# Sliding-window attention in a fused encoder step: probabilities divided ahead of their transposes, values as the stationary side, one pipeline stage more, and staging and sums on GpSimd

## What is computed

```python
def sink_attention(q, k, v, mask, sink):
    s = einsum('bnqhgd,bnkhd->bnhgqk', qg, k) * (HEAD_DIM ** -0.5)
    s = where(mask, s, -inf)
    mx = maximum(max(s, -1), sk)
    p = exp(s - mx)
    p = p / (sum(p, -1) + exp(sk - mx))
    o = einsum('bnhgqk,bnkhd->bnqhgd', p, v)
```

## Time and profile before

| | |
|---|---|
| Time, median of 3 runs | 2906.19 us (2901.15 to 2909.29) |
| Time of the profiled execution | 2909.79 us |
| Its span | 2908.0 us, 39590 instructions |
| TensorE's mean granted clock | 0.976 of full |
| Attention: first scores to the start of the output projection | 271.9 to 410.6 us |

### The profile page before, as it was taken

How to read it: one execution, slowest core, us unless ns; L and a number is a source line. 1 busy time by engine, 2 the same in 40 slices (tenths; PEclk the granted TensorE clock), 3 DMA queues, 4 the chain that set the end, 5 groups by cost and what they waited for, 6 DMA issues and landing times.

```text
span 2908.0 us, 39590 instructions
## 1 busy us (share of the span) xinstructions
PE 2795.7 (96%) x15799; PEld 2709.9 (93%) x15799; DVE 1076.5 (37%) x1476; ACT 541.0 (19%) x937; POOL 821.0 (28%) x584
## 2 busy tenths in 40 slices
PE   7999989999999999999899999989999999999995
PEld 7997769999999999999889898979999999999995
DVE  5127743422222221246645454552522222222225
ACT  3113631200110010022322314141201100100011
POOL 6542002322222222223122221342222222222231
PEclk9999979999999999999999999999999999999997
DMA  6321021111111111121233241432111111111111
GB/s 186 70 58 30 0 75 44 37 44 43 43 43 37 42 43 43 44 92 54 50 99 47 69 79 51 91 113 98 44 44 42 37 43 40 46 43 39 41 44 65
DMA packets 107099, 163.97 MB, mean 56 GB/s; under 512 B 55564, under 2 KB 66828, under 8 KB 106240
## 3 DMA queue, kind: packets, MB, share of 16 engines
q1 hardware_dynamic: 32368, 100.72, 12.5%
q10 hardware_dynamic: 74368, 60.93, 7.3%
q0 software_dynamic: 272, 0.98, 0.1%
HBM read 132.81 MB, written 24.49 MB: 54 GB/s over the span
## 4 chain that ended last, share of the span: by engine, by line
PE 84%; issue 9%; DVE 3%; POOL 2%; ACT 1%; DMA 0%; ACTq 0%; DVEq 0%; POOLq 0%
PE psum L572 76%; PE psum L671 2%; PE psum L794 1%; PE psum L599 1%; POOL w_lo L438 1%; PE psum L752 1%; PE psum L770 1%; POOL mid L522 1%; POOL w_hi L435 0%; PE psum L892 0%; DVE mid L1032 0%; DVE low L1526 0%; DVE a_lo L1169 0%; POOL mid L512 0%; PE psum L851 0%
## 5 line engine op out<-in xcount | busy, mean ns | idle before, releaser
L435 POOL TENSOR_SCALAR w_hi<-w_raw 128x1024 fp32r<-128x1024 f32 x191 | 204.5, 1071 | 1765.6 <-PE psum L572 1555.7
L572 PE MATMUL psum<-a_hi,w_hi 128*128 128x384 f32 x2808 | 655.4, 341 | 36.6 <-DVE a_lo L1020 16.9
L572 PE MATMUL psum<-a_lo,w_hi 128*128 128x384 f32 x2808 | 642.9, 336 | 0.0
L572 PE MATMUL psum<-a_hi,w_lo 128*128 128x384 f32 x2808 | 642.3, 336 | 0.0
L572 PEld LDWEIGHTS psum<-a_hi,w_hi 128*128 128x128 f32 x2808 | 502.0, 190 | 45.9 <-issue 22.8
L572 PEld LDWEIGHTS psum<-a_hi,w_lo 128*128 128x128 f32 x2808 | 505.1, 189 | 0.0
L572 PEld LDWEIGHTS psum<-a_lo,w_hi 128*128 128x128 f32 x2808 | 504.9, 189 | 0.0
L438 POOL TENSOR_TENSOR w_lo<-w_raw,w_hi 128x1024 fp32r<-128x1024 f32 x191 | 460.9, 2413 | 15.9
L1054 DVE TENSOR_TENSOR low<-psum,low 128x1152 f32<-128x1152 f32 x144 | 195.5, 1358 | 634.0 <-PE psum L572 633.9
L572 PE MATMUL psum<-h_hi,w_lo 128*128 128x384 f32 x1536 | 348.5, 334 | 0.0
L572 PE MATMUL psum<-h_hi,w_hi 128*128 128x384 f32 x1536 | 348.5, 334 | 0.0
(11 more groups left out here) (217 smaller groups left out, 2264.8 us busy)
## 6 DMA issues: line engine op xcount, KB each, us to landing
w_raw<-in_wall SPq DMA_DIRECT2D x191, 512.0 KB, 3.6
low<-in_x ACTq DMA_DIRECT2D x16, 576.0 KB, 9.0
high<-in_mem_in ACTq DMA_DIRECT2D x32, 257.0 KB, 4.7
out_mem_s<-high ACTq DMA_DIRECT2D x32, 257.0 KB, 3.1
out_x_spill<-low ACTq DMA_DIRECT2D x8, 576.0 KB, 2.7
low<-out_x_spill ACTq DMA_DIRECT2D x8, 576.0 KB, 7.0
out_y<-low ACTq DMA_DIRECT2D x8, 576.0 KB, 2.8
out_mix_spill<-mid ACTq DMA_DIRECT2D x3, 1152.0 KB, 5.4
```

What stands on the lines that cost most here:

```text
L435: nc.gpsimd.tensor_scalar(w_hi[:, s, :], w_raw[:, s, :], 1.0, 1.0, ALU.mult, ALU.mult)\
L572: r = mm(psum[:, z + i, 0:TN], w[:, s, k * P:(k + 1) * P], a[:, kk, tok(i)], start=first and n == 0, stop=last and n == 2)
```

## The change

Six edits go together. (1) The sums are finished on GpSimd (`denominators`), VectorE takes the reciprocal and multiplies the probabilities by it in place (`normalise`), before TensorE transposes them; `output` is gone. (2) In `weigh` the values are stationary with 64 columns and the transposed probabilities move, 128 columns; each key head writes its own half of the PSUM partitions, so that the result is already turned and `flip_out` is gone. (3) The sinks' exponentials take an argument that GpSimd has made (`sink_less_max`), so one activation does both heads. (4) `stage` moves to GpSimd, on all 128 partitions, with 0/1 masks in `halves`. (5) The stages stand at k = 0, 2, 3, 4 where they stood at k = 0, 1, 2, 3. (6) The steps are all written out.

The first three functions of the diff are GpSimd's, `normalise` is VectorE's, and the last activation is ScalarE's.

```diff
+            def stage(c, p):
+                n = 2 * c + p
+                if not first_two(n):
+                    pool.wait_ge(s_done, n - 1)
+                for v in range(2):
+                    r = nc.gpsimd.tensor_scalar(qs[:, v, 2 * p:2 * p + 2, :], qT[:, 2 * p:2 * p + 2, bass.ds(CH * c, CH)],
+                                                halves[:, v:v + 1], 1.0, ALU.mult, ALU.mult)
+                r.then_inc(q_staged, 1)
...
+            def sink_less_max(c, p):
...
+                pool.wait_ge(m_done, n + 1)
+                nc.gpsimd.tensor_tensor(st[:, p, 4:4 + width], st[:, p, 2:2 + width], cols[:, col:col + width], ALU.add)\
+                    .then_inc(sink_moved, 1)
...
+            def denominators(c, p):
...
+                pool.wait_ge(p_done, n + 1)
+                nc.gpsimd.tensor_tensor(st[:, p, 8:8 + width], st[:, p, 6:6 + width], st[:, p, 10:10 + width], ALU.add)\
+                    .then_inc(den_done, 1)
...
+                for k, part in ((-1, stage), (0, sink_less_max), (0, denominators)):
...
             def flip(c, p):
-                pe.wait_ge(p_done, n + 1)
+                pe.wait_ge(norm_done, n + 1)
...
-                    for v in range(2):
-                        for g, w, _, tile in parts:
-                            r = mm(psum[:, 6 + p, HD * v:HD * v + HD], pT[0:w, p, 2 * g + v, :],
-                                   v128[0:w, tile, HD * v:HD * v + HD], start=g == 0, stop=g == len(parts) - 1)
+                    for g, w, _, tile in parts:
+                        for v in range(2):
+                            h_ = slice(HD * v, HD * v + HD)
+                            r = mm(psum[h_, 6 + p, 0:P], v128[0:w, tile, h_], pT[0:w, p, 2 * g + v, :],
+                                   start=g == 0, stop=g == len(parts) - 1)
...
-            def flip_out(c, p):
-                pe.wait_ge(o_done, 2 * c + p + 1)
-                tr(psum[:, 6 + p, P:2 * P], (obs if is_sample(c) else ob)[:, p, :], ident).then_inc(ot_done, 1)
...
-                for k, stage in ((0, scores), (3, flip_out), (2, weigh), (1, flip)):
+                for k, stage in ((0, scores), (2, flip), (3, weigh)):
...
+            def normalise(c, p):
+                dve.wait_ge(den_done, n + 1)
+                V.reciprocal(st[:, p, 12:12 + width], st[:, p, 8:8 + width]).then_inc(rec_done, 1)
+                dve.wait_ge(rec_done, n + 1)
+                for v in range(width):
+                    a = pr[:, p, 192 * v:192 * v + w]
+                    r = V.tensor_scalar(a, a, st[:, p, 12 + v:13 + v], None, ALU.mult)
+                r.then_inc(norm_done, 1)
...
-                for k, part in ((0, maxima), (-1, stage), (1, denominators), (3, mixed_in), (2, output),
-                                (1, copy_last)):
+                for k, part in ((0, maxima), (1, normalise), (2, copy_last), (4, mixed_in)):
...
+                act.wait_ge(sink_moved, n + 1)
+                A(st[:, p, 10:10 + len(cells)], st[:, p, 4:4 + len(cells)], ACT.Exp).then_inc(p_done, 1)
...
-                for k, part in ((3, result_high), (0, probs), (1, copy_first)):
+                for k, part in ((2, copy_first), (4, result_high), (0, probs)):
```

More of the change, by code:

```diff
@@ L217, in build @@
         pT = take(2, 4, P)
-        ob = take(2, P)
-        obs = take(2, P)
         st = take(2, 16)
         nsink = mid[:, 4 * T + 2 * NB * P:4 * T + 2 * NB * P + 5]
+        halves = mid[:, 4 * T + 2 * NB * P + 5:4 * T + 2 * NB * P + 7]
         lnsq = uy.rearrange("p a g n -> p (a g n)")[:, 0:SQ_SLOTS * TN].rearrange("p (a b) -> p a b", a=SQ_SLOTS)
@@ L341, in is_sample, with result_place @@
             return isinstance(c, int) and c >= NCH
-        def result_places(c, p):
+        def result_place(c, p):
             if is_sample(c):
@@ L347, in result_places, with key_width @@
                 at = slice(TP + TB * b, TP + TB * (b + 1))
-                return [(h_, slice(0, 4), at, psum[h_, 6 + p, P + h_.start:P + h_.stop].rearrange(
-                    "p (j q) -> p j q", j=4)) for h_ in (slice(0, HD), slice(HD, P))]
-            return [(slice(0, P), slice(2 * p, 2 * p + 2), bass.ds(CH * c, CH),
-                     psum[:, 6 + p, P:2 * P].rearrange("p (j q) -> p j q", j=2))]
+                return slice(0, 4), at, psum[:, 6 + p, 0:HD].rearrange("p (j q) -> p j q", j=4)
+            return (slice(2 * p, 2 * p + 2), bass.ds(CH * c, CH),
+                    psum[:, 6 + p, 0:P].rearrange("p (j q) -> p j q", j=2))
         def attention_steps(engine, step):
-            for n in range(6):
+            for n in range(UNITS + 4):
                 step(n // 2, n % 2)
-            with engine.Fori(3, NCH) as c:
-                step(c, 0)
-                step(c, 1)
-            for n in range(2 * NCH, UNITS + 3):
-                step(n // 2, n % 2)
+        def key_width(c):
+            return CH * (c + 1) if isinstance(c, int) and c < 2 else 3 * CH
         def out3(b):
@@ L489, in _, with step @@
                 scaled(i)
+            def stage(c, p):
[7 more added lines that the diff above has]
+            def sink_less_max(c, p):
+                n = 2 * c + p
+                width, col = (1, C_SINKS) if is_sample(c) else (2, C_SINK + 2 * p)
+                pool.wait_ge(m_done, n + 1)
+                if not first_two(n):
+                    pool.wait_ge(p_done, n - 1)
+                nc.gpsimd.tensor_tensor(st[:, p, 4:4 + width], st[:, p, 2:2 + width], cols[:, col:col + width], ALU.add)\
+                    .then_inc(sink_moved, 1)
+            def denominators(c, p):
+                n, width = 2 * c + p, 1 if is_sample(c) else 2
+                pool.wait_ge(p_done, n + 1)
+                if not first_two(n):
+                    pool.wait_ge(norm_done, n - 1)
+                nc.gpsimd.tensor_tensor(st[:, p, 8:8 + width], st[:, p, 6:6 + width], st[:, p, 10:10 + width], ALU.add)\
+                    .then_inc(den_done, 1)
+            def step(c, p):
+                for k, part in ((-1, stage), (0, sink_less_max), (0, denominators)):
+                    u = earlier(c, p, k)
+                    if u and not (k == -1 and is_sample(u[0])):
+                        part(*u)
+            pool.wait_ge(rope_done, 2 * NT * 5)
+            pool.wait_ge(stat_done, NSINK)
+            stage(0, 0)
+            attention_steps(pool, step)
             single(U_OUT0 + 1, U_OUT0)
```

74 lines of the change are left out of this document (18 added, 56 removed).

## The result

The changed kernel takes 2867.44 us (median of 4 runs, 2864.37 to 2868.77) where the kernel before takes 2903.67 on the same chip (2900.86 to 2909.29): a ratio of 0.987, 95% interval 0.9856 to 0.9885. The forecast was 2891 with a range down to 2880. The sign was right, the size was not, and the time lies outside the range. The profiled execution took 2868.08 us with a span of 2866.3; against the profiled one of before that is 41.7 us less, where 15.6 were forecast. By the medians it is 36.2 us: the profiled execution of before was 3.6 us above the median of its runs.

What follows compares the result with a forecast made beforehand. TensorE was taken to bound the chunks' steps. Steps -11.6, start -4.0 and end 0 gave -15.6 us: 2909.8 to 2894.2 profiled, less 3.6 for the median, 2891 rounded; range 2880 to 2907.

Steps and rivals of the forecast that it cites:

- TensorE's time for a step after, 2.42 us: Attention's chunk steps: TensorE sets the step, 2.11 us of work plus 0.16 and 0.15, down from 2.865.
- issue left: TensorE's chunk step: 0.16 us of issue kept in each step, because the waits heading each part stay.
- The base of 2.865 us a step: Chunk steps of the kernel before: 74.49 us from unit's scores to first sample's scores, taken as 26 steps.
- passage: TensorE's chunk step: going from full-array work to half columns and back costs 0.15 us, bounds 0 and 0.30.
- The weighing is set by loading 128 stationary columns: Chunk steps' weighing: loaded columns set its 1.39 us; loading 64 and moving 128 makes it 0.87, 0.52 less.
- Rival D: Chunk steps: key heads' weighing overlaps, no switching cost, TensorE 1.9 to 2.0, VectorE bounds at 2.2; 2885 us; chance 0.08.
- the rule of the drain: TensorE's chunk step: changing tiling mode drains the engine, speaking against the change; step 2.27 us without, 2.57 with both sides.
- The start, -4.0: Attention's start: earlier value projection and shorter half-clock steps save 4.0 us; 2 if clock stays low longer, 9 if no fall.
- fifth stage: Attention's step pipeline: the extra stage costs nothing inside, since each part has more room to the next.
- The end, 0: Attention's end: alternating ScalarE and VectorE blocks stay, one more step is walked; 0 us, plus or minus 1.5.
- Ring and lock: Chunk steps: staging-to-sum wait cycle, 3.9 us per two steps, hidden; VectorE-GpSimd blocking adds nothing, up to 0.35 a step possible.
- rival C: TensorE waits more and its clock falls to half among the chunk steps; middle 2916 us; chance 0.17.

Runs made afterwards that it cites:

- weighing by head: Changed kernel with each key head's weighing products in a row, so neighbours mostly share a column half, against the kernel before: ratio 0.9934.

## Why the prediction was wrong

The step that failed is TensorE's time for a step after, 2.42 us, and in it the reason given for the weighing: that it is set by the columns loaded. The runs show 2.02 us. The weighing gains by where its neighbours lie, 0.28 us by their PSUM place and 0.43 by their column half, and the issue left in the sum belonged to the loop. Beside it terms at both ends were too small. In the profiled executions 26.1 us are missing from the forecast: 3.9 in the base of the chunks' steps and 10.7 in the step after, 4.7 at the start, 6.1 at the end, and 0.7 elsewhere.

**The base of 2.865 us a step.** Wrong by a count: between the scores at 297.17 and the first sample's lie 25 steps, not 26, and they start a unit later than I said. The 26 chunk steps of before took 78.39 us, 3.015 each, since some of them ran at half clock; at full clock a step is 2.885. This hid (3.015 - 2.865) x 26 = 3.9 us of the gain. Some 3 of these are the second fall of the clock, which no other kernel's trace has: to that extent the measured gain, too, is luck of the one execution. The rows also show one weighing, 1.39 us, of the two that alternate; the mean was 1.455.

**The step after, 2.42 us, measured 2.02.** Term by term:

| term | forecast | measured |
|---|---|---|
| weighing | 0.87 | 0.73 |
| issue left | 0.16 | 0 |
| transposes, scores and passage | 0.59 + 0.65 + 0.15 | 0.44 + 0.85 |

The differences are 0.14, 0.16 and 0.10, in all 0.40 us, or 10.4 over the 26 steps (10.7 with the 52.18 us that they took).

The *weighing* was nearly right in size and wrong in reason. "The weighing is set by loading 128 stationary columns" rested on one comparison, 0.174 against 0.163 a record, of records that differ in the accumulating, in the sharing of array columns and in the shape. The weighing by head shows that the swap alone gives nothing. That 0.87 lay near 0.73 is luck: the reason behind it is worth nothing, and one that the sum left out is worth 0.71. Had the diff's inner loop been written the other way round, my forecast would have been the same, and the attention 18 us longer. What counts is the order v inside g: different PSUM places 0.28, different column halves 0.43. Rival D had the mechanism, at a chance of 0.08, and TensorE's 1.9 to 2.0 with it; it failed in letting VectorE bind at 2.2, which is 1.95. The Trainium skill, TensorEngine Tiling (Array Packing), section Key Properties, says in the line below the one I used that different tiles can load and multiply in parallel. The traces agree, 0.73 us with two halves for 1.16 with one, places apart in both. I gave weight to the rule of the drain and not to its neighbour.

The *issue* of 0.16 stood in every second step only, belonged to the hardware loop and went with it. Its whole price was 0.235 us a step, more than the row named issue showed; with it, the full-clock step's gain adds up: loop 0.235, result's transpose 0.11, weighing 1.30 to 0.73, less 0.05 of passage, is 0.865 = 2.885 - 2.02.

The *passage* at 0.15 was the right size where it can be seen alone, in the transposes behind column halves. In the changed kernel the scores pay it (0.85 for 0.65), and the transposes, now behind scores, get 0.15 back; how much of this is only where a modelled end is drawn can't be told.

**The start, -4.0, measured -8.7.** The cause was named rightly, VectorE's wait beside the split, and the number was in the text ("9 if it does not fall"). I took the clock's half speed as given and costed little more than the wait. The split's move alone gives 5.95 us there, the staging on GpSimd 2.2 more. But what lets the clock come back early stays open: with the split moved it stayed low until 286 in before with the loop written out and until 288 in after without the fifth stage.

**The end, 0, measured -6.1.** The blocks "stay as they are", but the path runs through the units' steps between them, and these lost the output's two instructions and the result's transpose. The first block comes 4.02 us after the first sample's scores for 5.55, VectorE's first follows 0.3 us sooner on it, the two pairs are 1.45 us shorter each, the tail is 7.74 for 9.06 us: 1.5 + 0.3 + 2.9 + 1.3 = 6.0. In the gap ahead of VectorE's blocks the rows show the instructions that left (0.89 of the 1.45 us). For the gap ahead of ScalarE's, the first block and the tail only the place is shown; ScalarE's order it is not.

**The fifth stage "costs nothing inside".** True, and the wrong question. Without it the step is 2.875 us. I asked what each edit costs, not what the sum would be without it; the rows that I had give the ring of transposes, scores, maxima, the two small ones and `normalise`: 0.59 + 0.65 + 0.56 + 0.17 + 0.17 + 0.58 = 2.72 us before any handover.

**Ring and lock.** Both were right to leave out of the chunks' steps of after: staging 0.373 for 0.30 and multiplications 0.317 for 0.29 fit in the slack. But the ring does not have "0.9 to spare" over two steps: its parts in after's trace fill 4.04 us, twice 2.02, so a further GpSimd piece of 1.15 us in it costs 1.06 until the staging is taken out. The Trainium skill, SBUF — State Buffer, section Who interferes with whom, has the lock, and the 0.70 us row agrees with it. I looked for it in VectorE alone and among the chunks' steps. In the end of after it holds up GpSimd: each of VectorE's three blocks has a sum of one column beside it that takes 2.62 to 2.70 us for 0.19 and ends with the block. The first:

```profile
344.65 2.70 POOL L514 TENSOR_TENSOR mid<-mid 128x1 f32<-128x1 f32 x1 [2.99 <-ACT mid L1695]
```

The chain there is VectorE's, so this is not seen to cost time.

**The clock** did not fall among the chunks' steps (1.00 in 300 to 330); rival C was wrong. It stood at 0.50 in the end, from 344 to 374.

## What to carry to other kernels

Before a product's time is put down to columns loaded or moved, look at its neighbours: with the same shapes, eight records took 1.44 us here when neighbours added to the same place, 1.16 with the places apart, and 0.73 with the halves of the array's columns apart as well. Price a pipeline stage by summing each ring of waits with and without it, not by what the stage costs. Trace more than one execution before a stretch at half clock is put down to an edit. When a long block is moved under an engine that sets the step, cut it to below the slack of the engine that carries it and of those that share its port, and look where in a ring it lands.

## What the runs showed of the hardware beside this

- A hardware loop's cost can sit outside the row named issue: 0.235 us a step, of which the chain showed 0.16 us as issue in every second step (0.08 a step) and the rest as a longer weighing (1.39 and 1.52 us in turn for 1.30).
- The granted clock's recovery differs between kernels that look alike at the start: back within 278 to 280 us with the split moved and in after, not before 286 with the split moved and the loop written out, nor before 288 in after without the fifth stage. In 274 to 276 TensorE was busy 1.29, 1.54, 1.18 and 1.20 of 2 us; I can't say what decides.
- A product's eight f32 records (four instructions) take 1.44, 1.16 or 0.73 us by the place and the column half of their neighbours. An instruction of 128x1 or 128x2 on GpSimd or VectorE that takes 0.16 to 0.19 us alone took 0.70 to 2.70 beside a long one of the other engine, and ended with it.
- Writing out before's loop takes 10 us from a part of the program that it doesn't touch, 8 of them in the mLSTM between 1420 and 1780 us. Why stays open.
